# A depthwise convolution's diagonals built on ACT instead of GpSimd, its gating moved, and its layer norm shortened, in a two-block transformer kernel

## The reference, cut to what matters

```python
D_MODEL, SEQ, CONV_WIDTH_2, LN_EPS = 1024, 256, 31, 1e-5
def _conformer_conv(h, w_pw1, b_pw1, w_dw, b_dw, ln_g, ln_b, w_pw2, b_pw2):
    u = h @ w_pw1 + b_pw1                       # 1024 -> 2048
    u = u[..., :D_MODEL] * jax.nn.sigmoid(u[..., D_MODEL:])
    c = depthwise_conv(u, w_dw, taps=31, centred) + b_dw   # one weight per tap and channel
    c = jax.nn.silu(_layernorm(c, ln_g, ln_b))  # over the 1024 channels, eps 1e-5
    return c @ w_pw2 + b_pw2
```

## Time and profile before

| | |
|---|---|
| time, 3 runs | median 2341.53 us (2339.32 to 2342.05) |
| the profiled execution: its own time, its span | 2345.38 us, 2343.4 us |
| busy: PE, DVE, ACT, POOL | 2220.8, 1526.4, 963.7, 104.0 us |
| share of the span | 95%, 65%, 41%, 4% |
| mean granted clock of TensorE | 0.965 of full speed |
| the chain that ended last | PE 80%, DVE 14%, ACT 3% |

### The profile page before, as it was taken

How to read it: one execution, slowest core, us unless ns; L and a number is a source line. 1 busy time by engine, 2 the same in 40 slices (tenths; PEclk the granted TensorE clock), 3 DMA queues, 4 the chain that set the end, 5 groups by cost and what they waited for, 6 DMA issues and landing times.

```text
span 2343.4 us, 41745 instructions
## 1 busy us (share of the span) xinstructions
PE 2220.8 (95%) x17489; PEld 2157.5 (92%) x17489; DVE 1526.4 (65%) x2066; ACT 963.7 (41%) x1259; POOL 104.0 (4%) x54
## 2 busy tenths in 40 slices
PE   7999879999999999999999998889999999979998
PEld 6999768999999998899999997779999998969998
DVE  5777765777777646665465558967557556576555
ACT  3433433433533445443354343134435344544333
POOL 0000000000000000000000003610000000000000
PEclk9999887999999979999999999999999999989999
DMA  7776432777677431165445552214553553323552
GB/s 305 304 288 268 166 124 89 281 278 276 242 298 291 146 142 73 37 233 180 180 143 198 179 176 77 104 57 167 177 195 144 181 179 143 144 90 124 182 181 87
DMA packets 52940, 417.57 MB, mean 178 GB/s; under 512 B 5872, under 2 KB 6000, under 8 KB 6768
## 3 DMA queue, kind: packets, MB, share of 16 engines
q1 hardware_dynamic: 52848, 416.27, 48.0%
HBM read 415.20 MB, written 1.05 MB: 178 GB/s over the span
## 4 chain that ended last, share of the span: by engine, by line
PE 80%; DVE 14%; ACT 3%; issue 1%; DMA 1%; POOL 0%; DVEq 0%; SPq 0%; ACTq 0%
PE AB L272 15%; PE AB L273 15%; PE AB L274 15%; PE Y L272 9%; PE Y L273 9%; PE Y L274 9%; DVE lo L1639 3%; DVE qT L2354 2%; PE M L588 2%; PE M L541 1%; ACT hi L1173 1%; DMA ada_raw<-ada 1%; DVE ada_acc L1675 1%; PE Y L813 1%; PE N L854 1%
## 5 line engine op out<-in xcount | busy, mean ns | idle before, releaser
L1639 DVE TENSOR_TENSOR lo<-raw,hi 128x2048 fp32r<-128x2048 f32 x310 | 721.6, 2328 | 492.6 <-ACT hi L1173 492.5
L272 PE MATMUL AB<-h_hi,hi 128*128 128x256 f32 x3040 | 877.0, 288 | 14.1 <-DVE ada_raw L2364 5.7
L273 PE MATMUL AB<-h_lo,hi 128*128 128x256 f32 x3040 | 866.6, 285 | 0.0
L274 PE MATMUL AB<-h_hi,lo 128*128 128x256 f32 x3040 | 866.4, 285 | 0.0
L1173 ACT ACTIVATE hi<-raw 128x2048 fp32r<-128x2048 f32 x322 | 614.0, 1909 | 525.8 <-PE Y L274 278.6
L272 PEld LDWEIGHTS AB<-h_hi,hi 128*128 128x128 f32 x3040 | 589.9, 194 | 19.3 <-DVE ada_raw L2364 6.8
L273 PEld LDWEIGHTS AB<-h_lo,hi 128*128 128x128 f32 x3040 | 590.1, 194 | 0.2
L274 PEld LDWEIGHTS AB<-h_hi,lo 128*128 128x128 f32 x3040 | 589.9, 194 | 0.0
L272 PE MATMUL Y<-g_hi,hi 128*128 128x256 f32 x1280 | 362.2, 283 | 0.0
L273 PE MATMUL Y<-g_lo,hi 128*128 128x256 f32 x1280 | 362.2, 283 | 0.0
L274 PE MATMUL Y<-g_hi,lo 128*128 128x256 f32 x1280 | 362.2, 283 | 0.0
(11 more groups left out here) (341 smaller groups left out, 2258.6 us busy)
## 6 DMA issues: line engine op xcount, KB each, us to landing
raw<-slabs SPq DMA_DIRECT2D x322, 1024.0 KB, 4.8
ada_raw<-ada SPq DMA_DIRECT2D x35, 2048.0 KB, 8.1
kT<-ada SPq DMA_DIRECT2D x1, 1024.0 KB, 10.6
vt<-ada SPq DMA_DIRECT2D x1, 1024.0 KB, 12.6
x<-x_t SPq DMA_DIRECT2D x1, 1024.0 KB, 14.6
out_t<-x SPq DMA_DIRECT2D x4, 256.0 KB, 2.4
vec<-vectors SPq DMA_DIRECT2D x1, 462.0 KB, 4.1
hf<-constants SPq DMA_DIRECT2D x1, 401.0 KB, 14.6
```

Of the source, the lines that this page charges most:

```text
L272: nc.tensor.matmul(out_, w_hi, r_hi, start=start, stop=False, **kw)
L273: nc.tensor.matmul(out_, w_hi, r_lo, start=False, stop=False, **kw)
L274: return nc.tensor.matmul(out_, w_lo, r_hi, start=False, stop=stop, **kw)
L1639: nc.vector.tensor_tensor(lo[slot][:, :], raw[slot][:, :], hi[slot][:, :].bitcast(F32), ALU.subtract).then_inc(lo_done[slot], 1)
```

## The change

ACT now builds the diagonals, one Copy activation of 128x128 for each tap and chunk with the weights as the scale, in four buffers (two more in the unused half of `ada_raw`); POOL's `diagonals` goes. DVE's gating of chunk j+2 (with the slab preparation behind it) is issued at two thirds of pair j's taps instead of after them, for the chunks 2, 4 and 6. The last pair has 17 taps on DVE instead of 15, so PE has 14 instead of 16. The layer norm takes `deviation` and `root_of_sqrt`, sums all eight chunks of squares on PE without POOL's tree, reads the spread result from PSUM without a copy, interleaves `h_lo` with the scaling two chunks behind, and issues eight products of zeros behind `spread` instead of five. Two more table switches stand in ACT's program at other places: Sqrt before the squares, and Silu right after the root.

```diff
-        taps_dve = [DVE_TAPS] * (KD - 2) + [15, 15]
+        taps_dve = [DVE_TAPS] * (KD - 2) + [17, 17]
         diag = [a.rearrange("p t (n m) -> p (t n) m", m=P) for a in (vt, ot)]
+        diag += [ada_raw[:, 1, i * SLAB:(i + 1) * SLAB].rearrange("p (n m) -> p n m", m=P) for i in range(2)]
...
 # PE, conformer
-                        mm = nc.tensor.matmul(Y[:, k, :], diag[k % 2][:, tap - taps_dve[k], :],
+                        mm = nc.tensor.matmul(Y[:, k, :], diag[k % 4][:, tap - taps_dve[k], :],
...
-                stat_tree(hf)
+                s0 = c.take("sq", KD)
+                sums([(sq_ready, s0 + k + 1, hf[:, k, :]) for k in range(KD)], ones[1024])
+                spread(fill=(4, 8))
                 out_product()
...
 # POOL
-            def diagonals():
-
-                for k in range(KD):
-                    if k >= 2:
-                        pool.wait_ge(dw_part, k - 1)
-                    n = TAPS - taps_dve[k]
-                    w = v("w_dw", taps_dve[k] * KD, n * KD).rearrange("p (t k) -> p t k", k=KD)[:, :, k]
-                    nc.gpsimd.tensor_tensor(diag[k % 2][:, 0:n, :], ident[:, :].unsqueeze(1).to_broadcast([P, n, P]),
-                                            w.unsqueeze(2).to_broadcast([P, n, P]), ALU.mult
-                                            ).then_inc(diag_ready, 1)
...
 # ACT, conformer
+                def diagonals(k):
+
+                    if k >= 4:
+                        act.wait_ge(dw_part, k - 3)
+                    for tap in range(taps_dve[k], TAPS):
+                        ins = nc.scalar.activation(diag[k % 4][:, tap - taps_dve[k], :], ident[:, :], ACT.Copy,
+                                                   scale=v("w_dw", tap * KD + k))
+                    ins.then_inc(diag_ready, 1)
+
                 start_mixer()
                 for _ in range(3):
                     next_slab()
+                diagonals(0)
                 for j in range(8):
...
                     next_slab()
+                    if j:
+                        diagonals(j)
+                sqrt_table()
                 for k in range(KD):
                     act.wait_ge(cen_ready, k + 1)
                     nc.scalar.activation(hf[:, k, :], qT[:, k, :], ACT.Square).then_inc(sq_ready, 1)
+                deviation(ln_eps)
+                nc.scalar.activation(eps_[:, 1:2], eps_[:, 0:1], ACT.Silu)
                 operand()
...
 # DVE, conformer
+                def gated(j):
+
+                    dve.wait_ge(u_copied, c.take("cu") + 1)
+                    nc.vector.scalar_tensor_tensor(upad[:, j, 15:15 + T], bank()[:, 0:T], v("b_pw1", j),
+                                                   silu[:, (j % 2) * T:(j % 2 + 1) * T], ALU.add, ALU.mult
+                                                   ).then_inc(cu_done, 1)
+                    next_slab()
+
                 def taps(j):
 
                     n = taps_dve[j]
                     for tap in range(n):
+                        if tap == 2 * n // 3 and j + 2 < KD:
+                            gated(j + 2)
                         for k in (j, j + 1):
...
-                rstd_of(1e-5)
+                root_of_sqrt(1e-5)
+                dve.wait_ge(rstd_ready, c["stat"])
...
-                for k in range(KD):
-                    nc.vector.scalar_tensor_tensor(hf[:, k, :], qT[:, k, :], v("ln_g", k), rstd[:, :], ALU.mult,
-                                                   ALU.mult).then_inc(ln_u, 1)
-                for k in range(KD):
-                    dve.wait_ge(hh_ready, hh0 + k + 1)
-                    nc.vector.tensor_tensor(h_lo[:, k, :], kT[:, k, :], h_hi[:, k, :].bitcast(F32), ALU.subtract
-                                            ).then_inc(h_ready, 1)
+                for k in range(KD + 2):
+                    if k < KD:
+                        nc.vector.scalar_tensor_tensor(hf[:, k, :], qT[:, k, :], v("ln_g", k), N[:, 0:T], ALU.mult,
+                                                       ALU.mult).then_inc(ln_u, 1)
+                    if k >= 2:
+                        dve.wait_ge(hh_ready, hh0 + k - 1)
+                        nc.vector.tensor_tensor(h_lo[:, k - 2, :], kT[:, k - 2, :], h_hi[:, k - 2, :].bitcast(F32),
+                                                ALU.subtract).then_inc(h_ready, 1)
```

More of the change, by code:

```diff
@@ L1198, in begin, with deviation @@
                 ahead(2)
-            def deviation():
+            def deviation(eps=eps_):
                 act.wait_ge(stat_ready, c.take("stat") + 1)
-                nc.scalar.activation(root[:, :], M[:, 0:TT * WIDE:WIDE], ACT.Sqrt, bias=eps_[:, 0:1]).then_inc(sqrt_ready, 1)
+                nc.scalar.activation(root[:, :], M[:, 0:TT * WIDE:WIDE], ACT.Sqrt, bias=eps[:, 0:1]).then_inc(sqrt_ready, 1)
             def sqrt_table():
@@ L1556, in conformer @@
                         nc.scalar.activation(h_hi[:, k - 1, :], kT[:, k - 1, :], ACT.Copy).then_inc(hh_ready, 1)
-                c.take("stat")
                 sqrt_table()
@@ L1693, in begin @@
                 nc.vector.memset(eps_[:, :], EPS)
+                nc.vector.memset(ln_eps[:, :], 1e-5)
                 for n, t in ones.items():
@@ L1790, in root_of_sqrt @@
                 dve.wait_ge(sqrt_ready, c.take("sqrt") + 1)
[L1791 removed]
+                nc.vector.tensor_scalar(vh, M[:, 0:TT * WIDE:WIDE], eps, -0.5, ALU.add, ALU.mult).then_inc(dve_link, 1)
                 c.take("link")
@@ L2360, in taps @@
                         nc.vector.tensor_tensor(qT[:, k, :], qT[:, k, :], Y[:, k, :], ALU.add).then_inc(dw_done, 1)
-                for j in range(8):
-                    dve.wait_ge(u_copied, c.take("cu") + 1)
-                    nc.vector.scalar_tensor_tensor(upad[:, j, 15:15 + T], bank()[:, 0:T], v("b_pw1", j),
-                                                   silu[:, (j % 2) * T:(j % 2 + 1) * T], ALU.add, ALU.mult
-                                                   ).then_inc(cu_done, 1)
-                    next_slab()
-                    if j % 2:
-                        dve.wait_ge(cu_done, c["cu"])
-                        taps(j - 1)
+                gated(0)
+                for j in range(1, 8, 2):
+                    gated(j)
+                    dve.wait_ge(cu_done, c["cu"])
+                    taps(j - 1)
                 dve.wait_ge(mean_ready, 1)
```

10 lines of the change are left out of this document (4 added, 6 removed).

## The result

| | median us | lowest to highest | ratio to before, 95% |
|---|---|---|---|
| before | 2340.43 | 2338.93 to 2342.05 | |
| after | 2323.38 | 2319.83 to 2328.38 | 0.9929, 0.9907 to 0.9950 |
| before, measured again | 2342.04 | 2333.12 to 2344.29 | |
| after, measured again | 2323.26 | 2316.39 to 2326.56 | 0.9922, 0.9903 to 0.9941 |

The change makes the kernel 17 us faster (17.05, 0.7%), and about 19 where both were measured again.

What follows compares the result with a forecast made beforehand. DVE was taken to bound the convolution, stopped by POOL's diagonals. Terms 2.5 + 10.0 - 0.6 + 0 + 1.5 + 0.5 = 13.9 us, from a median of 2341.5 to 2327.6 us; 8-in-10 range 2321.5 to 2333.

Steps and rivals of the forecast that it cites:

- (a): Add ahead of the convolution: without POOL's early diagonals, DVE's stretched 128x1 pair and half `lo` shorten; gain 2.5 us.
- (b): Convolution: six `lo` without POOL gain 11.6 us, two more taps per chunk lose 1.6; net gain 10.0 us.
- (c): Mean behind the convolution: PE's last products run at the lower clock after 8 us of idleness; cost 0.6 us.
- (d): Layer norm's sums of squares, 32 records instead of 20: from 0.8 us lost to 3.3 gained by clock; taken as 0.
- (e): Layer norm's root, end of sums to first scaling: 3.41 us becomes 1.95, table load hidden; gain 1.5 us.
- rival 4: Silu table switch behind the layer norm's root has a drain, making the gain 0.7 us less: 2328.3 us; chance 3%.
- (f): Operand and first output slab: 1.6 us gained at full clock, 0.6 lost at the lower; middle taken, 0.5 gained.
- the one with a full clock: PE stays or comes back at full clock early, through mean, sums and slab: gain 18.9 us, 2322.6 us; chance 8%.
- The one with the lower level throughout: PE stays at the lower clock through sums, slab and a first-product stretch: gain 10.3 us, 2331.2 us; chance 6%.
- That the long `lo` were not POOL's: Convolution: PE's or ACT's writes lengthen `lo`, so 11.6 us stays: gain 2.3 us, 2339.2 us; chance 5%.
- ACT as the bound: Convolution: ACT reaches DVE's 21.7 us per pair at 0.77 us a diagonal; 2349 us at 1.0; chance 2%.

Runs made afterwards that it cites:

- experiment 1: Kernel before with only the diagonals moved to ACT in four buffers; gating, taps and layer norm as before: median 2327.61 us, ratio 0.9945.
- experiment 2: Changed kernel with the diagonals back on POOL, still in four buffers: median 2343.27 us, ratio 1.0022 to before.
- experiment 3: Changed kernel with the gating of chunks 2, 4 and 6 back behind the taps of the pair before: median 2325.67 us, ratio 0.9938.
- experiment 10: Changed kernel with 19 DVE taps for six chunks, 15 for the last two, zero products in PE's gaps, low part three chunks behind: 2309.61 us, ratio 0.9871.
- experiment 6: Changed kernel with thirty zero products on PE ahead of the mean's product of chunk 6: one execution, stretch between the two adds' roots 150.03 us (changed 152.93).
- experiment 9: Changed kernel with DVE taps 19 (first two chunks), 20 (four), 15 (last two), zero products in PE's gaps, low part three chunks behind: 2316.68 us, ratio 0.9892.
- experiment 8: Changed kernel with `h_lo` three chunks behind the scaling instead of two: one execution, stretch between the two adds' roots 152.25 us (changed 152.93).
- experiment 5: Changed kernel with five zero products instead of eight behind the layer norm's spread: one execution, stretch between the two adds' roots 152.87 us (changed 152.93).
- experiment 4: Changed kernel with the layer norm of before (Newton steps, POOL's tree, copy, separate loops, five zero products): median 2328.96 us, ratio 0.9945.
- experiment 7: Changed kernel with 15 instead of 17 DVE taps in the last pair: one execution, stretch between the two adds' roots 152.20 us (changed 152.93).

## Why the prediction was right

Its mechanism held: POOL's diagonals stopped DVE (experiments 1 and 2), and DVE alone bounded the convolution. Term by term, with the gain measured in the stretch behind each:

- **(a) early diagonals: 2.5, measured 3.28.** The 0.4 of the half `lo` and the 2.03 of the pair stood exactly. What I left out is 0.51 + 0.32: the late root kept PE idle for 2.8 us, and its four records that spread the root, and the sums after them, ran at the lower clock.
- **(b) convolution: 10.0, measured 10.08.** Shown in parts: POOL's relief 11.7 (experiment 1), two taps more -1.6, and the two waits that then open, 1.9, closed by the moved gates (experiment 3). ACT's diagonals came at 0.30 us each, under the 0.4 assumed, and PE's balance of 21.4 against 21.7 was so close that one tap more in each of the first six chunks used it up (experiment 10).
- **(c) mean: -0.6, measured -0.94.** The idle time (8 us forecast, 7.0 found) and the clock were right, the size wasn't: four records double from 1.13 to 2.08. Experiment 6 takes it back.
- **(d) sums of squares: 0, measured +0.35**, between the bounds of -0.8 and 3.3. The upper bound was worked out wrong: at full clock the sums do not only follow the squares, for 32 records at 0.12 are 3.84 us, from 1534.2 to 1538.0, which is 2.5 gained and not 3.3. Experiment 9 gets 2.46. Nor did the prediction see what the tree cost DVE beside it (4.37 against 2.77 for the subtractions).
- **(e) root: 1.5, measured 1.47**, in every kernel with the new layer norm. No drain showed around the table load, so rival 4 did not come. "ScalarE: Activation LUTs" of the Trainium skill (What ACT_TABLE_LOAD costs), which has one, is not borne out at this place: ACT's next instruction starts 0.02 us behind the load, and the load 0.02 behind the root.
- **(f) operand and first slab: 0.5, measured 1.24.** The last `h_lo` at 7.62 was as stepped through. The step that was off is the middle taken between two clocks: products that load PE half did not bring its clock down, and the sum at full clock, 10.9, was near the 11.23 found. The gain goes with the clock: the interleaving by itself made the last low part later, 7.62 against 6.76, and a lag of three gives 0.86 back (experiment 8). Nor do the extra zero products belong in it (experiment 5).

The terms sum to 15.5 instead of 13.9. That is 1.6 of the 4.2 us between forecast and median; another 1.1 is that before itself came out at 2340.43 beside it, instead of 2341.53; the remaining 1.5 lie within the scatter of either kernel's executions. That the time fell as near as it did owes something to luck, since terms (c), (d) and (f) hang on a clock that differs between executions.

The rivals: the one with a full clock (18.9, or 18.1 with the bound put right) did not come, but experiment 9 reaches its (c) and (d). The one with the lower level throughout did not come either: (d) and (f) gained 0.35 and 1.24 where it had them lose 0.8 and 0.6. That the long `lo` were not POOL's is refuted by experiments 1 and 2. ACT as the bound is excluded by the 0.30 us per diagonal against 0.77. Experiment 4 puts the new layer norm at 2.0, while (d), (e) and (f) as measured against before sum to 3.1: the 1.2 of (f) hangs on the clock and not on the layer norm alone.

Left open: why PE's clock falls to half, soon after the start of the convolution's first product and for some 3.4 us, in some executions of the same instructions and not in others. Of the eleven profiled executions without extra zero products there it fell in nine (before, the changed kernel twice, experiments 1, 2, 4, 5, 7 and 8) and did not in two (3 and 6); nor did it in the two that had them (9 and 10). That these products are the reason is not shown: two executions without them did the same.

## What to carry to other kernels

When an operation of an engine that is nearly idle on average overlaps the engine that bounds a stage, look at the durations of single instructions of the bounding one: its own rows may carry the other's cost, and moving the small work to a third engine with idle time can be worth more than the work itself. When a bound is relieved, ask at once which engine waits longer behind it, since PE's longer idle time here turned into a slower clock for the next 10 us; with products of zeros in the gaps the mean and the sums came 0.9 and 2.1 us sooner in experiment 9, together more than the taps shifted to PE gave (2.35). And compare executions between two fixed events around the change, not by their whole times.

## What the runs showed of the hardware

An instruction on POOL stretched DVE's beside it. A large one stretched even single-column instructions of DVE: two of 128x1 took 4.77 us in experiment 2, 2.38 in before and 0.35 alone. Small ones did too: beside three additions of 128x256 on POOL, three of DVE's eight subtractions of the same size took 0.95 us instead of 0.42. Which of the two engines stands still is not fixed: in experiment 2 POOL's 128x1408 lasted 7.86 us under taps that ran at their usual 0.40 (24 in 9.58), and ten us later one lasted 2.71 while fourteen taps took 2.3 us too long.

ACT's 128x128 copy with its scale from memory follows its predecessor after 0.30 us, though each one's own duration is 0.39: consecutive ones overlap, so what one costs in a row of them has to be read from the group's time and its count (11 in 3.31 us).

The granted clock falls or holds at the same place in different executions: PE fell after 3.69 us of idleness in experiment 7 and did not within 3.54 in experiment 3, and after 3.16 us of idleness the same product ran at 0.50 in experiment 1 and only part of the time below 1.00 (mean 0.72) in experiment 4. In the add ahead, 2.78 us of idleness were enough in before (the four records behind it took 1.23 us instead of 0.71), and in experiment 6 the clock fell with no more than 1.43 us of idleness at a time. The length of the last gap alone did not tell what the clock would be.
